# A hybrid decoder step on one core: who splits the recurrent layer's weights, where gates and values are taken, and how the last columns are cut

## The reference, cut to what matters

```python
def rglru_mixer(x, h0, conv_buf, ...):
    u = x @ w_in
    gate_branch, rec = u[..., :D_RNN], u[..., D_RNN:]
    xc = causal_dwconv(concatenate([conv_buf, rec]), conv_w, conv_b)      # width 4
    r = sigmoid(block_diag(xc, w_a, b_a)); i = sigmoid(block_diag(xc, w_x, b_x))
    log_a = -RG_C * r * softplus(-lam)
    a, mult = exp(log_a), sqrt(-expm1(2.0 * log_a))
    h = scan(a, mult * i * xc)
    return (h * gelu(gate_branch)) @ w_out, ...

def conv_ffn(x, ...):
    val, gate = split(causal_dwconv(x @ w_up, ...))                       # width 3
    return (gelu(gate) * val) @ w_down

# attention: p = softmax(q @ k + bias) for two branches, w = p0 - lam * p1, out = w @ v
# output: rmsnorm(x, final_norm)
```

## Time and profile before

| | us |
|---|---|
| median of 3 runs | 2657.1 (2655.6 to 2657.28) |
| the profiled execution | 2657.53 |
| its span | 2655.4 |
| PE busy / DVE busy / POOL busy / ACT busy in the span | 2600.1 / 1453.0 / 833.3 / 704.1 |
| mean granted TensorE clock | 0.993 |

### The profile page before, as it was taken

The page is one execution under the profiler, slowest core; times in us unless marked ns, Lnnn a source line. Parts: engine busy times, 40 slices in busy tenths (PEclk is TensorE's granted clock), DMA queues, the critical chain, the costliest instruction groups (busy, mean ns, idle before and its releaser), DMA issues.

```text
span 2655.4 us, 40398 instructions
## 1 busy us (share of the span) xinstructions
PE 2600.1 (98%) x16892; PEld 2539.0 (96%) x16892; DVE 1453.0 (55%) x2302; ACT 704.1 (27%) x1172; POOL 833.3 (31%) x458
## 2 busy tenths in 40 slices
PE   8899999999999999999999999899999999999997
PEld 8899999999999999998999998799999999999997
DVE  8766375444444445476556555636445544444448
ACT  5555031111111111124444444512111111111112
POOL 2332333233233233334333333023233323323321
PEclk9999999999999999999999999999999999999999
DMA  4111311111111111134233232311111111111112
GB/s 148 44 35 32 121 47 41 48 47 41 49 48 41 47 48 45 43 122 131 83 103 99 95 96 92 134 52 41 48 48 43 45 48 43 46 48 48 40 48 80
DMA packets 81922, 170.05 MB, mean 64 GB/s; under 512 B 9509, under 2 KB 47909, under 8 KB 81486
## 3 DMA queue, kind: packets, MB, share of 16 engines
q1 hardware_dynamic: 75790, 145.18, 17.2%
q10 hardware_dynamic: 5952, 22.30, 2.2%
HBM read 145.93 MB, written 26.23 MB: 65 GB/s over the span
## 4 chain that ended last, share of the span: by engine, by line
PE 89%; DVE 6%; ACT 3%; issue 1%; POOL 0%; DMA 0%; DVEq 0%; SPq 0%; ACTq 0%; POOLq 0%
PE psum L803 70%; PE psum L997 3%; PE psum L999 3%; PE psum L1001 3%; PE psum L1053 2%; PE psum L1029 2%; PE psum L1041 1%; PE psum L1233 1%; DVE line L1812 1%; DVE line L1772 1%; PE psum L1112 0%; DVE y L1964 0%; DVE xn_lo L1829 0%; DVE xn_lo L1972 0%; PE psum L1085 0%
## 5 line engine op out<-in xcount | busy, mean ns | idle before, releaser
L803 PE MATMUL psum<-xn_hi,w_hi 128*128 128x352 f32 x3024 | 655.9, 325 | 4.5 <-DVE xn_lo L1972 1.8
L803 PE MATMUL psum<-xn_lo,w_hi 128*128 128x352 f32 x3024 | 652.2, 323 | 0.0
L803 PE MATMUL psum<-xn_hi,w_lo 128*128 128x352 f32 x3024 | 651.5, 323 | 0.0
L693 POOL TENSOR_SCALAR w_hi<-w_raw 128x1024 fp32r<-128x1024 f32 x172 | 188.4, 1095 | 1445.8 <-PE psum L803 1343.6
L803 PEld LDWEIGHTS psum<-xn_hi,w_hi 128*128 128x128 f32 x3024 | 515.6, 189 | 8.0 <-POOL w_lo L697 2.9
L803 PEld LDWEIGHTS psum<-xn_lo,w_hi 128*128 128x128 f32 x3024 | 519.6, 188 | 0.0
L803 PEld LDWEIGHTS psum<-xn_hi,w_lo 128*128 128x128 f32 x3024 | 514.0, 188 | 0.0
L697 POOL TENSOR_TENSOR w_lo<-w_raw,w_hi 128x1024 fp32r<-128x1024 f32 x172 | 444.2, 2582 | 14.3
L1492 ACT ACTIVATE line<-line,columns 128x1072 f32<-128x1072 f32 x96 | 123.4, 1285 | 1057.3 <-DVE line L1795 1057.3
L1836 DVE TENSOR_TENSOR x<-psum,x 128x1056 f32<-128x1056 f32 x192 | 241.3, 1257 | 250.0 <-PE psum L803 246.0
L1790 DVE TENSOR_TENSOR line<-psum,inverse_rms 128x704 f32<-128x704 f32 x102 | 91.0, 892 | 463.4 <-PE psum L803 463.2
(11 more groups left out here) (272 smaller groups left out, 2961.7 us busy)
## 6 DMA issues: line engine op xcount, KB each, us to landing
w_raw<-in_w SPq DMA_DIRECT2D x200, 512.0 KB, 3.5
k_pages<-in_cache_k SPq DMA_DIRECT2D x128, 64.0 KB, 2.1
v_pages<-in_cache_v SPq DMA_DIRECT2D x128, 64.0 KB, 2.2
scratch_line<-scratch_row ACTq DMA_DIRECT2D x1, 4608.0 KB, 21.0
x<-in_x SPq DMA_DIRECT2D x8, 528.0 KB, 8.5
scratch_x<-x ACTq DMA_DIRECT2D x1, 4224.0 KB, 12.7
out_k<-raw ACTq DMA_DIRECT2D x8, 528.0 KB, 2.7
out_v<-raw ACTq DMA_DIRECT2D x8, 528.0 KB, 3.5
```

The lines of the kernel that those rows point to most:

```text
L693: pool.tensor_scalar(WHI[:, s], WRAW[:, s], 1.0, 0.0, ALU.mult, ALU.add).then_inc(w_hi, 1)
L803: last = pe.matmul(PS[:, 3 * (a % 2) + c, 0:CH], w[:, s, k, :], r[:, c * CH:(c + 1) * CH], start=start and first, stop=stop and final)
```

## The change

1. Recurrent layer: units 4 to 15 are split by ScalarE (`weights_high(u)`) and VectorE (`weights_low(u)`), placed in their queues, and no longer by GpSimd, which goes on with unit 16.
2. `rec_conv` is cut in two: `gate(n-2)` now stands between the first passes and the last (for n = 4, ahead of all); `input_gate` stands ahead of `xc_low`. The temporary of the convolution is a line of its own (`CONVT`, at the end of Y), so `tap(3)` needn't wait for a scan, and `recurrence` not for `xc_ready`.
3. ScalarE runs a one-column Gelu ahead of `tanh_a`, so that tanh is taken from the gelu table, and a one-column Sqrt ahead of the last squares.
4. Attention: the values are transposed at the end of step 1, the samples' weights at the end of step 2, the outputs at the end of steps 6 and 7; the fill isn't cut. `values_out` goes to the end of ScalarE's step 1.
5. The end: the last two units' high and low parts lie on `XC1`, `XCH`, `XCL` and the gate weights' place; the first doesn't wait of its own for the last up product, the second waits for the last `h_lo`. The pieces have 400, 400 and 256 columns. The first spread comes two pieces later; VectorE's outputs of the first part all fall beside the last part.

Left out below are hunks that only put the new widths in the place of `CH` and `QC`.

```diff
-def ahead(g):
-    n = filled(g) - filled(g - 1)
-    return n // 2 if g % 8 in (2, 6, 7) else 0
 def beside_scores(g):
...
             order.append((("scores", h), None, None, None, ("output", h), ("turned", h))[t])
+        if g < STEPS and t == 1:
+            order += [("v", h, 0), ("v", h, 1), ("v", h, 2)]
         if g < STEPS and t == 2:
-            order += [("v", h, 0), ("v", h, 1), ("v", h, 2), ("weights", h)]
+            order.append(("weights", h))
         if g < STEPS and h and t >= 6:
...
 FINAL = 5 * KT
-QC = CH // QUARTERS
+FLO = (0, 400, 800)
+FW_ = (400, 400, 256)
+def final_cols(c):
+    return slice(FLO[c], FLO[c] + FW_[c])
+def root_cols(c):
+    return slice(FLO[c] // QUARTERS, (FLO[c] + FW_[c]) // QUARTERS)
...
+        CONVT = at("conv_tmp", [P, LINEW], F32,
+                   n0 - 4 * LINEW)
         HHI = at("h_hi", [P, 4, T], F32R, a0)
         HLO = at("h_lo", [P, 4, T], F32R, a0 + 16 * T)
-        PICKS = at("first_rows_apart", [P, QUARTERS, P], F32, l0 + 4 * 4 * LINEW)
-        W2HI = at("last_w_hi", [P, 2, KT, P], F32R, n0)
-        W2LO = at("last_w_lo", [P, 2, KT, P], F32R, n0 + 8 * KT * P)
         def region(lo, hi):
...
             return place
+        PICKS = at("first_rows_apart", [P, QUARTERS, P], F32, l0 + 4 * 4 * LINEW)
+        wr = region(c0, c1)
+        W2HI = [wr(f"last_w_hi{s}", [P, KT, P], F32R) for s in range(2)]
+        W2LO = [wr("last_w_lo0", [P, KT, P], F32R), region(g0, top[0])("last_w_lo1", [P, KT, P], F32R)]
...
-            return Z[2] if n else Z[6]
+            return CONVT if n else Z[6]
...
                 gates(n)
-            for n in range(3, KT):
-                straight(unit_rec(n), unit_rec(n) + 1)
-                gates(n - 1)
-                straight(unit_gate(n - 2), unit_gate(n - 2) + 1)
-            gates(KT - 1)
-            straight(unit_gate(KT - 2), U_OUT)
+            for n in range(2, KT):
+                gates(n)
+            pool.wait_ge(w_lo, U_OUT)
             straight(U_OUT, U_OUT + 2)
...
             ffn(U_F1, F_UNITS - 2)
-            pool.wait_ge(acc_done, up_acc(A_F1, GROUPS - 1, 3) + 1)
             for u in (NU - 2, NU - 1):
                 s = u % 2
+                if s:
+                    pool.wait_ge(FS[1]["hl_ready"], 2 * GROUPS)
                 pool.wait_ge(w_in[s], 16 * (u // 2 + 1))
-                pool.tensor_scalar(W2HI[:, s], WRAW[:, s], 1.0, 0.0, ALU.mult, ALU.add
+                pool.tensor_scalar(W2HI[s][:, :, :], WRAW[:, s], 1.0, 0.0, ALU.mult, ALU.add
                                    ).then_inc(w_hi, 1)
                 pool.wait_ge(w_hi, u + 1)
-                pool.tensor_tensor(W2LO[:, s], WRAW[:, s], W2HI[:, s].bitcast(F32), ALU.subtract
-                                   ).then_inc(w_lo, 1)
+                pool.tensor_tensor(W2LO[s][:, :, :], WRAW[:, s], W2HI[s][:, :, :].bitcast(F32),
+                                   ALU.subtract).then_inc(w_lo, 1)
...
                     sample_turn(h)
-                fill(ahead(g))
-                if t == 2:
-                    turn_values(h)
-                    sample_weights(h)
-                if h and t >= 6:
-                    turn_output(h - 1, t - 6)
-                fill(filled(g) - filled(g - 1) - ahead(g))
+                fill(filled(g) - filled(g - 1))
                 if g == STEPS - 4:
...
                     project(g - (STEPS - 4), 0, (0, 1))
+                if t == 1:
+                    turn_values(h)
+                if t == 2:
+                    sample_weights(h)
+                if h and t >= 6:
+                    turn_output(h - 1, t - 6)
             pe.wait_ge(sosq_done, 1)
...
                     pe.wait_ge(FS[1]["hl_ready"], 2 * g + 2)
-                    whi, wlo = ((WHI, WLO), (W2HI, W2LO))[e]
+                    whi, wlo = ((W2HI[u % 2], W2LO[u % 2]) if e else
+                                (WHI[:, u % 2], WLO[:, u % 2]))
                     for t in range(2):
...
                             end = e == groups[-1] and t == 1 and r is HLO
-                            last = pe.matmul(PS[:, z, 0:CH], w[:, u % 2, k, :], r[:, h, cols],
+                            last = pe.matmul(PS[:, z, 0:FW_[c]], w[:, k, :], r[:, h, cols],
                                              start=first, stop=end)
...
+                n = FW_[c] // QUARTERS
                 for j in range(QUARTERS):
-                    lo = c * CH + QC * j
-                    last = pe.matmul(PS[32 * j:32 * (j + 1), z, 0:QC], ONES[:, 0:32],
-                                     line[:, lo:lo + QC], start=first, stop=end)
+                    lo = FLO[c] + n * j
+                    last = pe.matmul(PS[32 * j:32 * (j + 1), z, 0:n], ONES[:, 0:32],
+                                     line[:, lo:lo + n], start=first, stop=end)
                 if end:
...
                     final_sums(0, 6, Z[2], True, True)
-                if n == final_index(1, 6):
+                if n == final_index(2, 0):
                     final_spread(0, 7)
...
             def weights_high(u):
-                act.wait_ge(w_in[u], 16)
-                act.activation(WHI[:, u], WRAW[:, u], ACT.Copy).then_inc(w_hi, 1)
+                s = u % 2
+                act.wait_ge(w_in[s], 16 * (u // 2 + 1))
+                if u >= 2:
+                    act.wait_ge(w_hi, u)
+                    wait_acc(act, AFTER[u - 2] - 1)
+                act.activation(WHI[:, s], WRAW[:, s], ACT.Copy).then_inc(w_hi, 1)
...
                 wait_read(act, acc_diag(n))
-                if n < KT - 1:
-                    act.wait_ge(xc_ready, n + 2)
                 act.activation(Z[2][:, 0:T], Z[6][:, 0:T], ACT.Tanh, scale=SP2[:, n:n + 1],
...
             tanh_x(0)
+            weights_high(4)
             tap(1)
...
             tanh_a(1)
+            weights_high(5)
             tanh_x(1)
...
             recurrence(1)
-            tanh_a(2)
-            gelu(1)
-            act.wait_ge(h_done, 3)
-            tap(3)
-            tanh_x(2)
-            xc_high(3)
-            recurrence(2)
-            for n in range(4, KT):
+            for n in range(3, KT):
+                if n > 3:
+                    weights_high(2 * n)
                 tap(n)
+                if n == 3:
+                    weights_high(2 * n)
+                weights_high(2 * n + 1)
+                act.activation(CARRY[:, 9:10], EPSC[:, :], ACT.Gelu_apprx_tanh)
                 tanh_a(n - 1)
...
                 recurrence(n - 1)
+            act.activation(CARRY[:, 9:10], EPSC[:, :], ACT.Gelu_apprx_tanh)
             tanh_a(KT - 1)
...
                     weights_back(g - 2)
-                if t == 2:
-                    values_out(h)
                 exponentials(g)
...
                     square_sum(g - 4)
+                if t == 1:
+                    values_out(h)
                 if h and t == 4:
...
                 act.wait_ge(fin_mm, c + 1)
-                act.activation(RQ[:, QC * c:QC * (c + 1)], PS[:, z, 0:QC], ACT.Sqrt, bias=EPSC[:, :],
-                               scale=1.0 / D).then_inc(fin_root, 1)
+                act.activation(RQ[:, root_cols(c)], PS[:, z, 0:FW_[c] // QUARTERS], ACT.Sqrt,
+                               bias=EPSC[:, :], scale=1.0 / D).then_inc(fin_root, 1)
+            act.activation(CARRY[:, 9:10], EPSC[:, :], ACT.Sqrt)
             for c in range(NCH):
...
             def weights_low(u):
+                s = u % 2
+                if u >= 2:
+                    dve.wait_ge(w_lo, u)
                 dve.wait_ge(w_hi, u + 1)
-                dve.tensor_tensor(WLO[:, u], WRAW[:, u], WHI[:, u].bitcast(F32), SUB
+                dve.tensor_tensor(WLO[:, s], WRAW[:, s], WHI[:, s].bitcast(F32), SUB
                                   ).then_inc(w_lo, 1)
...
+            def rec_taps(n):
+                return [col(C_RGW + j * KT + n) for j in range(RW)]
+            def rec_conv_first(n):
+                dve.wait_ge(rec_tap, n + 1)
+                conv_first(REC, taps_line(n), rec_taps(n), None, RW - 1)
             def rec_conv(n):
-                XC, S_ = XCS[n % 2], taps_line(n)
-                dve.wait_ge(rec_tap, n + 1)
-                taps = [col(C_RGW + j * KT + n) for j in range(RW)]
-                conv_first(REC, S_, taps, None, RW - 1)
-                conv_last(REC, S_, XC, taps, RW - 1, xc_ready)
+                conv_last(REC, taps_line(n), XCS[n % 2], rec_taps(n), RW - 1, xc_ready)
                 dve.tensor_copy(RTAIL[:, n, 0, :], REC[:, SEQ:SEQ + RW - 1])
...
             series()
+            rec_conv_first(0)
             rec_conv(0)
...
             neg_lambda()
+            rec_conv_first(1)
             rec_conv(1)
+            weights_low(4)
             xc_low(1)
...
             scan(0)
+            weights_low(5)
+            rec_conv_first(2)
             rec_conv(2)
...
             gate(1)
+            weights_low(6)
             scan(1)
+            weights_low(7)
+            rec_conv_first(3)
             rec_conv(3)
...
```

(15 more changed lines are left out.)

25 lines of the change are left out of this document (13 added, 12 removed).

## The result

| | before | after |
|---|---|---|
| median of five runs, us | 2657.28 (2655.6 to 2658.39) | 2642.43 (2639.28 to 2642.79) |
| the profiled execution, us | 2657.53 | 2642.79 |
| its span, us | 2655.4 | 2641.0 |
| PE / DVE / POOL / ACT busy, us | 2600.1 / 1453.0 / 833.3 / 704.1 | 2594.8 / 1450.3 / 784.3 / 711.3 |

The ratio is 0.9941, with a 95% interval of 0.993 to 0.9952; the forecast was 2640, between 2631 and 2651.

What follows compares the result with a forecast made beforehand. TensorE was taken as the bound (89% of the span). Recurrent layer -11.9, attention -3.5 and end -1.6 gave -17.0 us from 2657.5, so 2640.5, stated as 2640 since the runs' median is 0.4 lower; range 2631 to 2651.

Steps and rivals of the forecast that it cites:

- Removed waits and clock: Recurrent layer: four TensorE waits go, 13.1 us, and the clock lost behind the long ones returns, 4.0 us.
- ScalarE's split ahead of the table load: Recurrent layer: the split delays table load and `tanh_a`, so a unit waits 0.92 us, five times, 4.6 us added.
- `weights_high(4)`: Recurrent layer: this ScalarE split delays the first chain, which already costs 0.54 us, by some 0.3 us more.
- VectorE's twelve low parts: Recurrent layer: twelve `weights_low` at 1.24 us each fit into VectorE's waits and cost nothing; without that cover 1.2 each.
- Attention, seven heads: Attention: the 0.29 us wait for the values' copy and three fill restarts of about 0.08 go: 0.53 x 7 = 3.7 us.
- Last head: Attention's last head, no fill left as cover: waits go and come, taken as 0 us, between -3 and +3.
- The end: Last products and output transfers: shorter waits, VectorE becomes the bound, narrower transfer saves 0.5; -1.6 us, bounds +1 and -4.
- (a): Recurrent layer rival: table load hidden, or ScalarE's split never holds `tanh_a`; 4.6 us better, 2635.5; chance 0.11.
- (b): Recurrent layer rival: half the gain comes, another wait or clock loss remains; 6 to 10 us worse, 2648; chance 0.14.
- (c): Recurrent layer rival: the ScalarE and VectorE chain sets the pace, only 5 us or less gained; 2652 or more; chance 0.07.
- (d): Recurrent layer rival: each table load also has the Trainium skill's drain, 5 x 1.38 = 6.9 us worse, 2647; chance 0.03.
- (e): Attention rival: the value turn at step 1's end finds ScalarE busy in every head; slower, 2682; chance 0.03.

Runs made afterwards that it cites:

- experiment 1: Two edits of the changed kernel: VectorE's old order with the new splits (2648.11 us), or units 4 to 15 split by GpSimd with the new order (2640.91 us).
- experiment 3: Attention edits of the changed kernel: output transposes mid-fill in steps 6 and 7, 2639.6 us; value turn mid-fill in step 1, 2641.24; at step 2's end, 2652.46.
- rg_gpsimd_splits: The changed kernel with units 4 to 15 split by GpSimd again, VectorE's new order kept: 2640.91 us.
- rg_gate_behind: The changed kernel with VectorE's old order (gate behind the whole convolution), splits kept on ScalarE and VectorE: 2648.11 us.
- end_splits_late: The changed kernel with both of the last two weight splits on GpSimd behind the last `h_lo`, not only the second: 2638.45 us.
- attn_output_in_fill: The changed kernel with the output transposes of steps 6 and 7 back in the middle of the fill: 2639.6 us.

## Why the prediction was right, point by point

The profiled execution came out at 2642.8 us, 2.3 above the sum of 2640.5. The recurrent layer was 0.1 worse than forecast, attention 1.8, nearly all of it in the last head, and the end 0.4. The mechanism was right in the recurrent layer, where 11.76 of the 14.4 us are; that its size agrees to 0.1 us is in part luck, as the second and third points say.

- **Removed waits and clock** (13.1 + 4.0). All four waits went, and both slow stretches. Right, and so is the division of causes: experiment 1 brings one wait back with the order and leaves the other to the blocking.
- **ScalarE's split ahead of the table load** (five times 0.92). Five waits at the predicted place; the idle time is 0.70 and, with the restart behind it, a pair and a `diag` take 27.40 us (97.78 to 125.19) instead of the 26.55 that the earlier trace rows give without the clock's part (131.16 to 158.03, less 0.32): 0.85. The term was 0.07 too large, as the tiny Gelu delays `tanh_a` by 0.11 us and not 0.2.
- **`weights_high(4)`** (0.3) cost 0.93 (1.47 against 0.54): it stands ahead of `tap(1)` and the whole chain behind it waits for its 1.05 us. `gate(2)`'s thin margin (0.3) cost nothing. Together 5.2 again, by luck: three errors cancel, in 5 x 0.85 + 0.93 + 0 instead of 5 x 0.92 + 0.3 + 0.3.
- **VectorE's twelve low parts** cost nothing in the changed kernel, as said; only when ScalarE was made earlier did one of them (ahead of `gate(2)`) show, with 0.52 us.
- **Attention, seven heads** (3.7): 3.46. The size was right, but its split into 0.29 and three restarts of 0.08 was not: cutting the fill costs 0.03 us a head at most. The 0.29 is seen to go; the other 0.19 comes with the turn's place too (experiment 3), by what isn't shown.
- **Last head** (0, between -3 and +3): +1.74 in the profiled run. Both effects of the working are in the trace: the scores of step 2 start 2.5 us later (1645.62, where the old order shifted by 14.98 would give 1643.12), and the wait for `sample_weights` grows from 0.67 to 2.86. But see the section after next: kernels with the same code there differ by more than the 1.74.
- **The end** (-1.6): -1.16, of which -2.78 up to the last spread and +1.62 behind it. The step that failed is the transfer: 656 columns instead of 704 should have saved 0.5, and the profiled run has a straggling transfer instead. Even without the straggling nothing was saved: 9.07 and 9.11 us from the last spread to the end, against 9.03 in the kernel before. That VectorE becomes the bound was right (4.00 of 4.00 busy, 2.25 us wait), and so was the 0.8 for the tail copies; the first spread waits no more, but the second does, 0.84.
- **The rivals.** (a) fell: the load isn't hidden. (b) and (c) fell. (d) fell. The load of 1.28 us is followed 1.30 us after its start by the next activation, without the drain that the Trainium skill states ("ScalarE: Activation LUTs", "What ACT_TABLE_LOAD costs"). (e) did not come. It also misread its row: the 1.02 us of the earlier trace rows were released by VectorE (`o_q`), not by ScalarE. What the copies cost in step 2, 1.90 us per head, is another mechanism: there they wait for TensorE's turn and hold the exponentials behind them.

## What to carry to other kernels

Work moved to an idle engine isn't free there if it stands ahead of something that another engine waits for: a table load or a wait-free operation belongs ahead of the wait, and the moved operation behind the urgent one. Look for very small VectorE operations with durations of microseconds beside GpSimd's two-operand passes: they point to lost time that a new order alone doesn't mend (3.13 us of wait were left in `rg_gpsimd_splits`). Before widths are made unequal, add up what every engine does per piece, since the narrow piece is bound by the engine whose work doesn't shrink with it (here VectorE, with 2.25 us of wait ahead of the last sums).

## What the runs showed of the hardware that I had not expected

**The price of a wait in granted clock didn't rise with its length.** Behind the wait of 6.18 us the products lost 1.54 us, behind 4.88 it was 2.44, behind 4.39 (`rg_gate_behind`) 2.61, and behind 3.13 (`rg_gpsimd_splits`) still 1.43, though the first triple there took a normal 0.76. Before these runs the bound that I had was only that waits up to 1.12 cost none (nor did the 1.47 of the changed kernel). The window behind the 3.13 shows 0.57 (second block), that is, most of it at 1.2 instead of 2.4 GHz. The waits themselves show where the rest went: within the 6.18 and the 4.88 of the kernel before (first block) the granted clock was already 0.75 and 0.88, so part of the low stretch passed while TensorE stood still, while within the 3.13 it was 1.00.

```profile
122.20:128.30 6.10, 0.00 (x0) 0.00 (x0) 6.03 (x7) 3.20 (x3) 0.78 (x1) 0.75 0.23 86
183.00:187.80 4.80, 0.00 (x0) 0.00 (x0) 4.76 (x5) 2.40 (x3) 3.31 (x2) 0.88 0.11 8
```

```profile
152.00:156.00 4.00, 4.00 (x17) 4.00 (x17) 3.97 (x7) 2.93 (x3) 0.00 (x0) 0.57 0.42 135
156.00:160.00 4.00, 4.00 (x27) 4.00 (x26) 0.82 (x1) 3.96 (x4) 0.00 (x0) 1.00 0.00 0
```

**The same last head took from 74.50 to 77.36 us.** Its instructions are the same in these kernels, and so are its waits up to the 2.86; in the two kernels below, those behind it agree too, to 0.04 us. What differs between the two is how long the granted clock is low. Windows of the changed kernel (77.36) and of `end_splits_late` (74.50), the clock being the third number from the end:

```profile
1645.00:1655.00 10.00, 6.89 (x43) 4.83 (x42) 4.34 (x16) 5.23 (x14) 0.00 (x0) 0.83 0.74 263
1655.00:1665.00 10.00, 7.15 (x71) 5.89 (x70) 8.98 (x24) 8.25 (x19) 0.00 (x0) 0.66 0.01 2
```

```profile
1645.00:1655.00 10.00, 5.76 (x43) 4.16 (x43) 5.91 (x21) 5.76 (x16) 0.00 (x0) 1.00 0.71 257
1655.00:1665.00 10.00, 8.30 (x89) 6.92 (x90) 8.59 (x25) 8.88 (x20) 0.00 (x0) 0.83 0.30 95
```

The others with that code lie at 75.55 to 75.97 in seven kernels and once more at 77.20. So a difference of 1.7 us there, such as the +1.74 of the table, says little of the edit.

**The last transfer ended in one of two ways.** From the last spread to the end it took 9.07 and 9.11 us in three kernels and 10.64 to 10.73 in the others of the same widths; with 352 columns it was 9.03 and 9.17 in two and 10.69 in two. In the long case the transfer runs at full rate and then a remainder trickles for some 2 us; the last 3 us of the changed kernel and of `attn_output_in_fill` (last two numbers: share of the DMA engines, GB/s):

```profile
2638.00:2641.00 3.00, 0.00 (x0) 0.00 (x0) 0.00 (x0) 0.00 (x0) 0.00 (x0) 0.50 0.10 32
```

```profile
2634.20:2637.20 3.00, 0.00 (x0) 0.00 (x0) 0.00 (x0) 0.00 (x0) 0.00 (x0) 0.50 0.62 213
```

What decides between the two wasn't found. The low clock in the last head (1.7 us) and this (1.6) would together give about the spread of the changed kernel's own executions, 2639.28 to 2642.79; only one of them has a trace, so that isn't shown.
